# State space decays of a two-block transformer kernel: one 64-row product for the high and low sums, a maximum on VectorE with a broadcast operand, and the chunk's own sum as the bias of the exponential

## The reference

```
SSM_N_GROUPS, heads per group, SSM_CHUNK = 8, 4, 128      # 32 heads, 4 chunks
a_cum = cumsum(a within a chunk)                          # a <= 0, per head
seg = a_cum[..., :, None] - a_cum[..., None, :]           # t, s
decay_in = exp(where(causal, seg, -inf))
cb = einsum('bctgn,bcsgn->bgcts', cc, bc)
y_diag = einsum('bgcts,bgrcts,bcsgrp->bctgrp', cb, decay_in, xc)
decay_to_end = exp(a_cum[..., -1:] - a_cum)
chunk_decay  = exp(a_cum[..., -1])
y_off = einsum('bctgn,bcgrpn,bgrct->bctgrp', cc, entering, exp(a_cum))
```

## Time and profile before

| | us |
|---|---|
| median of 3 runs | 1713.52 |
| lowest and highest | 1710.45, 1713.75 |
| the profiled execution, its own time | 1713.32 |
| its span | 1711.5 |
| TensorE busy | 1667.8 (97%) |
| VectorE busy | 998.4 (58%) |
| ScalarE busy | 821.8 (48%) |
| GpSimd busy | 683.4 (40%) |

### The profile page before, as it was taken

One profiled execution on the slowest core, in us unless ns is written; L12 is line 12 of the kernel. 1 busy time (PEld: TensorE's weight loads), 2 busy tenths in 40 slices (PEclk: granted clock), 3 DMA queues, 4 the chain that ended last, 5 costly groups with the idle time before them and its releaser, 6 DMA issues.

```text
span 1711.5 us, 23401 instructions
## 1 busy us (share of the span) xinstructions
PE 1667.8 (97%) x8968; PEld 1348.9 (79%) x8968; DVE 998.4 (58%) x1881; ACT 821.8 (48%) x1379; POOL 683.4 (40%) x889
## 2 busy tenths in 40 slices
PE   8999899999999999988999999999999999999998
PEld 8987567977988888867877777877788777787876
DVE  6498773533575756697656666067453554445445
ACT  6564752632654445335464444155455453534434
POOL 5454423422414251343455556455442333324440
PEclk9999999999999999999999999999999999999999
DMA  8423001211313142302221222211211311212201
GB/s 301 168 89 114 25 1 50 88 61 50 124 49 137 62 146 74 123 23 89 99 69 56 74 74 74 96 56 52 93 64 52 100 52 61 67 51 86 69 28 55
DMA packets 24807, 137.03 MB, mean 80 GB/s; under 512 B 2511, under 2 KB 5839, under 8 KB 11000
## 3 DMA queue, kind: packets, MB, share of 16 engines
q1 hardware_dynamic: 24696, 135.53, 22.9%
HBM read 133.40 MB, written 2.12 MB: 79 GB/s over the span
## 4 chain that ended last, share of the span: by engine, by line
PE 85%; DVE 8%; ACT 5%; issue 2%; DMA 0%; SPq 0%; DVEq 0%; ACTq 0%
PE ps L1630 81%; PE ps L1634 3%; ACT whi L2163 1%; DVE CT L2890 1%; DVE tmp L2646 0%; ACT L2163 0%; PE ps L1638 0%; ACT XH L2163 0%; ACT tmp L2163 0%; DVE XL L2719 0%; DVE R L2890 0%; DVE LNS L2679 0%; DMA MEM<-memT 0%; DVE LG L2646 0%; DVE XL L2723 0%
## 5 line engine op out<-in xcount | busy, mean ns | idle before, releaser
L3263 POOL TENSOR_TENSOR wlo<-raw,whi 128x256 fp32r<-128x256 f32 (+1 forms) x804 | 607.6, 793 | 850.6 <-ACT whi L2163 850.6
L2163 ACT ACTIVATE whi<-raw 128x2048 fp32r<-128x2048 f32 (+4 forms) x147 | 254.6, 1736 | 159.9 <-PE ps L1630 103.9
L1630 PE MATMUL ps<-XH,whi 128*128 128x512 f32 (+1 forms) x1176 | 299.2, 375 | 4.4 <-ACT XH L2163 4.3
L1630 PE MATMUL ps<-XL,whi 128*128 128x512 f32 (+1 forms) x1176 | 281.5, 361 | 0.0
L1630 PE MATMUL ps<-XH,wlo 128*128 128x512 f32 (+1 forms) x1176 | 281.2, 361 | 0.0
L1630 PEld LDWEIGHTS ps<-XH,whi 128*128 128x128 f32 x1176 | 201.4, 190 | 43.8 <-ACT XH L2163 7.0
L1630 PEld LDWEIGHTS ps<-XL,whi 128*128 128x128 f32 x1176 | 205.2, 189 | 34.6
L1630 PEld LDWEIGHTS ps<-XH,wlo 128*128 128x128 f32 x1176 | 205.5, 190 | 34.1
L2750 DVE TENSOR_TENSOR R<-ps,R 128x512 f32<-128x512 f32 (+1 forms) x80 | 51.0, 637 | 133.4 <-PE ps L1630 132.8
L1630 PE MATMUL ps<-BH,whi 128*128 128x512 f32 (+1 forms) x320 | 89.4, 397 | 0.0
L1630 PE MATMUL ps<-BL,whi 128*128 128x512 f32 (+1 forms) x320 | 84.2, 380 | 0.8 <-DVE BL L3190 0.8
(11 more groups left out here) (384 smaller groups left out, 3010.3 us busy)
## 6 DMA issues: line engine op xcount, KB each, us to landing
raw<-wall SPq DMA_DIRECT2D x107, 1024.0 KB, 4.8
raw<-wall SPq DMA_DIRECT2D x11, 512.0 KB, 3.5
raw<-wall SPq DMA_DIRECT2D x8, 576.0 KB, 3.7
raw<-wall SPq DMA_DIRECT2D x4, 768.0 KB, 4.2
BFL<-scr SPq DMA_DIRECT2D x2, 1024.0 KB, 6.7
outN<-Y SPq DMA_DIRECT2D x8, 256.0 KB, 2.1
MEM<-memT SPq DMA_DIRECT2D x2, 512.0 KB, 5.0
XTA<-x SPq DMA_DIRECT2D x2, 512.0 KB, 9.4
```

Of the source, the lines that this page charges most:

```text
L1630: return nc.tensor.matmul(o_, l, r_, start=start, stop=stop, skip_group_check=True)
L2163: return nc.scalar.activation(o_, i_, func, bias=bias, scale=scale)
L3263: t = tt(wlo[u % NSPL][:, c], raw_of(u)[:, c], f32(whi[u % NSPL][:, c]), ALU.subtract)
```

## The change

- The high and low sums stand in one tile `ACS` of 64 partitions: `ACS[0:32]` from ACT and `ACS[32:64]` from DVE. `IDR` has 64 rows, twice the negative unit matrix (two small ACT copies, moved into `dc0`). `sx` has one product of 64 rows where it had two of 32; what it leaves in PSUM is -a_cum[t].
- `NAC`, -a_cum with the tokens in the partitions, takes the place of `ACUM`.
- DVE has one operation on 512 columns for each head where it had four on 128: `max(-a_cum[t], -a_cum[s])`, with `NAC` broadcast along t.
- ACT's exponential into `ECG` gets the scale -1. In place of one exponential on the 512 columns of `ESG` there are four on 128 columns, with the scale -1 and the column of `NAC` of the chunk as the bias: exp(-max(-a_cum[t], -a_cum[s]) - a_cum[s]).

```diff
-        IDR = sb("IDR", [32, 32], F32R, at=rw_at)
-        ACH = sb("ACH", [32, T], F32R, at=stat_at)
-        ACL = sb("ACL", [32, T], F32R, at=stat_at + 2048)
-        ACUM = sb("ACUM", [128, 4, 32], at=kt_at + 2048)
+        IDR = sb("IDR", [64, 32], F32R, at=rw_at)
+        ACS = sb("ACS", [64, T], F32R, at=stat_at)
+        NAC = sb("NAC", [128, 4, 32], at=kt_at + 2048)
...
             def sx(g, h):                                            # TensorE
                 hd = 4 * g + h
-                one_ = IDR[:, hd:hd + 1].to_broadcast([32, 128])
                 o_ = taken(e, "sx", g, h)
                 e.wait_ge(*on("a_dc", "dc1"))
                 e.wait_ge(*on("d_dc", "dc1"))
-                mm(o_[:, :], one_, ACH[:, :], True, False)
-                mm(o_[:, :], one_, ACL[:, :], False, True).then_inc(S("p_sx"), 1)
+                mm(o_[:, :], IDR[:, hd:hd + 1].to_broadcast([64, 128]), ACS[:, :], True, True).then_inc(S("p_sx"), 1)
...
+            def dc0():                                               # ScalarE
+                for r in (0, 32):
+                    act(IDR[r:r + 32, :], ident[r:r + 32, r:r + 32], ACT.Copy, scale=-1.0).then_inc(S("a_dc"), 1)
...
-                act(ACUM[:, :, :], o_[:, 256:384].rearrange("p (c h) -> p c h", c=4), ACT.Copy).then_inc(S("a_dc"), 1)
+                act(NAC[:, :, :], o_[:, 256:384].rearrange("p (c h) -> p c h", c=4), ACT.Copy, scale=-1.0).then_inc(S("a_dc"), 1)
...
-                act(ACH[:, :], slot("dc", 2)[0:32, :], ACT.Copy).then_inc(S("a_dc"), 1)
-                act(IDR[:, :], ident[0:32, 0:32], ACT.Copy).then_inc(S("a_dc"), 1)
+                act(ACS[0:32, :], slot("dc", 2)[0:32, :], ACT.Copy).then_inc(S("a_dc"), 1)
 
             def sx(g, h):                                            # ScalarE
                 e.wait_ge(*on("d_sx", "sx", g, h))
-                act(ECG[:, h, :], slot("sx", g, h)[:, 128:T], ACT.Exp).then_inc(S("a_sx"), 1)
-                act(ESG[:, h, :], ESG[:, h, :], ACT.Exp).then_inc(S("a_sx"), 1)
+                act(ECG[:, h, :], slot("sx", g, h)[:, 128:T], ACT.Exp, scale=-1.0).then_inc(S("a_sx"), 1)
+                for c in range(4):
+                    cc = slice(128 * c, 128 * c + 128)
+                    act(ESG[:, h, cc], ESG[:, h, cc], ACT.Exp, NAC[:, c, 4 * g + h:4 * g + h + 1], -1.0).then_inc(S("a_sx"), 1)
...
-                tt(ACL[:, :], slot("dc", 2)[0:32, :], f32(ACH[:, :]), ALU.subtract).then_inc(S("d_dc"), 1)
+                tt(ACS[32:64, :], slot("dc", 2)[0:32, :], f32(ACS[0:32, :]), ALU.subtract).then_inc(S("d_dc"), 1)
 
             def sx(g, h):                                            # VectorE
...
-                for c in range(4):
-                    cc = slice(128 * c, 128 * c + 128)
-                    ts(ESG[:, h, cc], o_[:, cc], ACUM[:, c, hd:hd + 1], 0.0, ALU.subtract, ALU.min).then_inc(S("d_sx"), 1)
+                tt(ESG[:, h, :].rearrange("p (c t) -> p c t", c=4), o_[:, :].rearrange("p (c t) -> p c t", c=4),
+                   NAC[:, :, hd:hd + 1].to_broadcast([128, 4, 128]), ALU.max).then_inc(S("d_sx"), 1)
```

More of the change, by code:

```diff
@@ L850, in program @@
                                                             ("close", ("cv", h, d), [("d_cvv", d + 1)]))]),
-            "dc0": lambda: one({"p_dc": 1, "d_dc": 2}, ("dc", 0), "ps", "d_dc"),
-            "dc1": lambda: ({"p_dc": 2, "a_dc": 5, "d_dc": 1},
+            "dc0": lambda: one({"p_dc": 1, "a_dc": 2, "d_dc": 2}, ("dc", 0), "ps", "d_dc"),
+            "dc1": lambda: ({"p_dc": 2, "a_dc": 4, "d_dc": 1},
                             [("open", ("dc", 1), "ps"), ("close", ("dc", 1), [("a_dc", 3)]),
                              ("open", ("dc", 2), "ps"), ("close", ("dc", 2), [("d_dc", 0)])]),
-            "sx": lambda g, h: one({"p_sx": 1, "d_sx": 4, "a_sx": 2}, ("sx", g, h), "ps", "a_sx", 1),
+            "sx": lambda g, h: one({"p_sx": 1, "d_sx": 1, "a_sx": 5}, ("sx", g, h), "ps", "a_sx", 1),
             "gate": lambda g: ({"a_gate": 6}, []),
@@ L2631, in scalar_program @@
             play(dict(init=init, mem=mem, split=split, hb=hb, hs=hs, rb1=rb1, sq=sq, rs=rs, ap=ap, nm=nm, al=al, pj=pj, bt0=bt0, bt1=bt1, ix=ix, va=va,
-                      ex=ex, tu=tu, rc=rc, ss=ss, kl=kl, vl=vl, mv=mv, uv=uv, ce=ce, ct=ct, cv=cv, dc1=dc1, sx=sx,
+                      ex=ex, tu=tu, rc=rc, ss=ss, kl=kl, vl=vl, mv=mv, uv=uv, ce=ce, ct=ct, cv=cv, dc0=dc0, dc1=dc1, sx=sx,
                       gate=gate, g0=g0, g2=g2, g3=g3, g4=g4, lq=lq, lt=lt, kn=kn, vv=vv, zs=zs, qk=qk, pt=pt, pv=pv, fo=fo, fr=fr))
```

## The result

| | before | after |
|---|---|---|
| median, us | 1713.63 (4 runs) | 1734.89 (4 runs) |
| lowest and highest | 1710.45, 1717.07 | 1733.33, 1736.41 |
| the profiled execution, its own time | 1713.32 | 1734.98 |
| its span | 1711.5 | 1733.2 |

The changed kernel takes 1.0129 times as long (95% interval 1.0117 to 1.0141): 21.3 us slower, where 16.5 were forecast. The direction and the delays on ScalarE came as predicted. The size is at the upper edge of the range: 1734.89 where the range ended at 1735, and as a ratio 1.0129 where 1735 to 1713.5 is 1.0125. What filled the difference was not in the forecast.

A forecast was written before the change was run, and what follows sets the result against it. The prediction took TensorE as the bound, with a slackless chain from ScalarE over VectorE beside it; group losses of 1.55 to 2.55 us summed to 16.5 us slower, TensorE's 7.3 us saving included, giving 1730 us, range 1722 to 1735.

The forecast's parts named there:

- What bounds the kernel: Whole span: TensorE, busy for 97%, so a removed product is worth its full spacing if nothing else is then late.
- the second chain: From decays' end to last chunk, ScalarE to VectorE to TensorE: no slack at its end; 2.55 us lost in groups 2, 3, 5.
- The rival of the gate alone: At the last chunk: no wait, groups lose only what the gate takes, 12.3 us in all, giving 1726; chance 20%.
- TensorE's product: `sx` products on TensorE: 32 go, four a group, saving 0.91 us a group, 7.3 us in all.
- ScalarE: Decays: small exponentials 0.29 us apart, block 6.25 us against 3.72, late by about 2.55 us in groups 2 to 6.
- The two rivals by another spacing: Small exponentials on ScalarE: full 0.40 us each, giving 1744, chance 5%; or 0.17 us apart, giving 1714.5, chance 8%.
- the row of 0.17: Profile row: two ScalarE operations on 128 columns without a tile bias start 0.17 us apart; used as bound from below.
- The start of ScalarE brought forward in groups 0, 1 and 7: Decays: ScalarE starts earlier by 0.4 us in groups 0 and 7, 0.6 in group 1.
- VectorE's part: Decays on VectorE: 16 operations a group become four, ending 1.5 us or more earlier; worth nothing in groups 2 to 6.
- the small edits: Moved `IDR` copies, one copy gone from `dc1`, and `NAC` for `ACUM`: costed at nothing.
- What this does at the gate: Group 2, product with `CTs`: TensorE waits 2.57 us and gains 0.91, net 1.66 us slower.
- My list of what would show it: Trace signs: 0.29 spacing, 6.2 us block, gate waits near 2.6 us in groups 2 to 6, `STT` waits about 0.9.

The follow-up runs named there:

- e5: Kernel before, with one 64-row product per head and the scan step issuing `GY` and `BL` last in a group's turn (except beside group 4): 1709.67 us, ratio 0.9989.
- e11: Kernel before, with only the scan step issuing `GY` and `BL` moved last in a group's turn (except beside group 4): 1712.62 us, ratio 1.0001.
- e3: Changed kernel, four exponentials of 128 columns kept but without the bias from a tile (own sum left out): 1719.77 us, ratio 1.0038.
- e4: Changed kernel, with overwritten filler products on TensorE before it waits for the gate: 1729.47 us, ratio 1.0098 against the kernel before.
- e2_one_exp: Changed kernel, with one exponential of 512 columns per head and the chunk's own sum left out: 1709.51 us, ratio 0.9982 against the kernel before.

## Why the prediction was right or wrong

- *What bounds the kernel, and the second chain:* right. TensorE waits at the gate in all eight groups, and in the groups without a fall of the clock the loss is that of the two chains within 0.07 us: 1.7 where only the gate counts (group 4), 2.55 where the last chunk passes the whole delay on (group 5), 2.2 between them (group 6). The rival of the gate alone is out.
- *TensorE's product:* right at 0.91 from the first product of the sums to the projection behind them, 934.64 - 932.60 = 2.04 us before and 939.76 - 938.65 = 1.11 after in group 2. Of a whole group 0.8 to 0.9 is left, seen in e5 against e11 in groups 1 to 5, where nothing else is late.
- *ScalarE:* right. Spacing 0.29, block 6.29 for 6.25. The two rivals by another spacing fall with it; the row of 0.17 was for reads from PSUM, and on this tile even without a bias it is 0.20 (e3): that rival's condition, a bias that costs nothing, was wrong, and its spacing too.
- *The start of ScalarE brought forward in groups 0, 1 and 7, VectorE's part, the small edits:* right by the sum. e4 has 1.74, 1.52 and 1.76 there.
- *"What this does at the gate":* wrong in size, and this is the step that failed. It priced the new wait at its own length, and nowhere in the sum or the range does the clock of TensorE stand. The term that was missing is the granted clock behind a wait: 2.2 us in group 0 (wait 3.77), 0.6 each in groups 2 and 3, 1.2 in group 7, in sum 4.5 of the 5.2 us missed in the profiled execution. Another 0.6 is the first stretch, which differs by more than that between executions of one program. e4 shows it: with the waits filled with work the forecast's own sum comes out.
- *The range:* that the measured median lies right at its end of 1735 is luck. That end was made for a spacing of 0.33 us, and the spacing was 0.29; the time came there by the clock.
- *My list of what would show it:* the delay at the gate is right, 950.97 - 938.65 = 12.32 us from the `sx` products to the one with `CTs`, against 943.26 - 932.60 = 10.66, 1.66 more. But I looked for a wait of 2.6 us, and the two of the gate are 1.99 together. The stop itself is as long as forecast, 12.32 less the 10.66 - 0.93 = 9.73 us of work that is left, or 2.59; I take it that the missing 0.6 lies in the modelled ends of the products before each wait, which count as busy. The waits for `STT` are 1.0 us where I said 0.9, in groups 2 and 3 only when the clock does not fall, and in group 1 (1.0) and group 6 (0.5), which the list did not name.

## What to carry to other kernels

A new wait of TensorE costs its length and, where the clock has been full through the stretch, perhaps a fall of the clock behind it: here 0.5 to 2.2 us more for waits of 2 to 4 us, in some executions and not in others, so it belongs in the range, upward only. To split one ScalarE operation so that a per-chunk number fits in as a bias costs a start for each piece (0.20 us from one to the next, 0.29 with the bias, where the whole of 512 columns took 0.52), which no saving on an engine beside it gives back if ScalarE feeds the next stage. And a product saved on the busiest engine is worth little (here nothing that could be measured) until the chain that meets it at the end of the group has been loosened as well.

## What the runs showed of the hardware that I had not expected

- A fall of the clock is not fixed by the program. The changed kernel fell behind the gates of groups 0, 2, 3 and 7 in one execution and of 0, 2, 3, 5, 6 and 7 in another, with equal waits at the gate. Groups 0 and 7, with the longer waits (3.77 and 2.51 us), fell in both.
- In group 0 a wait of 1.10 us left the clock full in the kernel before; one of 1.20 us in e2_one_exp was followed by a clock of 0.63 from 866 to 870 us. Whether the tenth of a microsecond or the place in time decides, no run separates.
- Products that do nothing but keep TensorE at work ahead of a wait made the kernel 5 us faster (e4 against the changed kernel).
